# Two issuers for the expert weights: down blocks from GpSimd's queue, up blocks from SyncE's

## What is computed

```
def swiglu(h, w1, w3, w2):
    return (jax.nn.silu(h @ w1) * (h @ w3)) @ w2

def moe_swiglu(h, w_router, w1, w3, w2):
    logits = jnp.einsum('bsd,de->bse', h, w_router)
    top_val, top_idx = lax.top_k(logits, TOP_K)                 # 2 of 8
    top_w = jax.nn.softmax(top_val, axis=-1)
    gates = jnp.sum(one_hot(top_idx, 8) * top_w[..., None], axis=-2)
    out = zeros
    for e in range(8):
        out = out + gates[..., e:e + 1] * swiglu(h, w1[e], w3[e], w2[e])
```

## Time and profile before

| | us |
|---|---|
| median of 3 runs (lowest, highest) | 1298.56 (1297.44, 1298.94) |
| the profiled execution, its own time | 1295.39 |
| its span, first to last instruction | 1293.6 |
| mean granted PE clock over the span | 0.996 |
| expert stage, first block used to last block used | 453.9 to 1282.0 |

### The profile page before, as it was taken

One profiled execution on the slowest core, in us unless ns is written; L12 is line 12 of the kernel. 1 busy time (PEld: TensorE's weight loads), 2 busy tenths in 40 slices (PEclk: granted clock), 3 DMA queues, 4 the chain that ended last, 5 costly groups with the idle time before them and its releaser, 6 DMA issues.

```text
span 1293.6 us, 29466 instructions
## 1 busy us (share of the span) xinstructions
PE 1251.1 (97%) x13303; PEld 732.9 (57%) x13303; DVE 382.4 (30%) x484; ACT 246.3 (19%) x328; POOL 23.0 (2%) x38
## 2 busy tenths in 40 slices
PE   9999999999999999999999999999799999999775
PEld 6998888888999833453433643453243453355222
DVE  4777644444667520111120111002012002011102
ACT  5654543333573300000000000000000000000001
POOL 3000000000100000000000000000000000000000
PEclk9999999999999999999999999999999999999998
DMA  9842745523746899999999999999999999999994
GB/s 312 297 158 98 265 176 174 182 97 116 277 168 235 348 413 404 407 365 414 411 411 412 414 409 413 413 411 411 415 411 412 411 408 406 412 414 397 409 411 202
DMA packets 115972, 430.74 MB, mean 333 GB/s; under 512 B 10615, under 2 KB 17047, under 8 KB 101378
## 3 DMA queue, kind: packets, MB, share of 16 engines
q1 hardware_dynamic: 114226, 423.48, 83.5%
q0 software_dynamic: 1616, 5.33, 1.2%
HBM read 427.72 MB, written 2.11 MB: 332 GB/s over the span
## 4 chain that ended last, share of the span: by engine, by line
PE 87%; DMA 11%; DVE 1%; ACT 1%; issue 0%; SPq 0%; POOL 0%; POOLq 0%; DVEq 0%
PE psum L1907 34%; PE psum L1927 17%; PE psum L1428 9%; PE psum L1430 9%; PE psum L1429 9%; DMA ring<-in_moe_w 9%; PE psum L1644 1%; DMA ring<-in_moe_w_end 1%; PE psum L1881 1%; PE psum L1964 1%; PE psum L1856 1%; PE psum L1447 1%; PE psum L1780 0%; PE psum L1603 0%; PE psum L1604 0%; DMA x<-in_x 0%
## 5 line engine op out<-in xcount | busy, mean ns | idle before, releaser
L1907 PE MATMUL psum<-ring,xe 128*32 128x512 f32 (+1 forms) x5376 | 518.8, 541 | 18.5 <-DMA ring<-in_moe_w 13.5
L1907 PEld LDWEIGHTS psum<-ring,xe 128*32 128x32 f32 x5376 | 168.9, 110 | 348.1 <-issue 271.0
L1927 PE MATMUL psum<-ring,gT 128*32 128x256 f32 x4640 | 259.0, 379 | 9.0 <-DMA ring<-in_moe_w 9.0
L1927 PEld LDWEIGHTS psum<-ring,gT 128*32 128x32 f32 x4640 | 148.1, 110 | 123.3 <-issue 17.2
L1287 DVE TENSOR_TENSOR gate<-gate,psum 128x768 f32<-128x768 f32 (+3 forms) x32 | 24.5, 767 | 511.0 <-ACT gate L831 511.0
L926 DVE TENSOR_TENSOR wlo<-raw,whi 128x2048 fp32r<-128x2048 f32 (+1 forms) x66 | 145.3, 2228 | 58.7 <-ACT whi L657 58.7
L831 ACT ACTIVATE gate<-psum 128x768 f32<-128x768 f32 (+3 forms) x32 | 21.2, 661 | 611.0 <-PE psum L1907 611.0
L657 ACT CAST whi<-raw 128x2048 fp32r<-128x2048 f32 (+1 forms) x66 | 120.2, 1861 | 56.8 <-PE psum L1430 32.5
L1428 PE MATMUL psum<-whi,f_hi 128*128 128x512 f32 (+1 forms) x320 | 123.8, 387 | 1.0 <-DVE wlo L926 0.9
L1430 PE MATMUL psum<-whi,f_lo 128*128 128x512 f32 (+1 forms) x320 | 121.4, 379 | 0.0
L1429 PE MATMUL psum<-wlo,f_hi 128*128 128x512 f32 (+1 forms) x320 | 121.3, 379 | 0.0
(11 more groups left out here) (249 smaller groups left out, 774.1 us busy)
## 6 DMA issues: line engine op xcount, KB each, us to landing
ring<-in_moe_w SPq DMA_DIRECT2D x384, 512.0 KB, 14.9
ring<-in_moe_w SPq DMA_DIRECT2D x112, 1024.0 KB, 18.3
raw<-in_ffn_w SPq DMA_DIRECT2D x33, 1024.0 KB, 5.7
ring<-in_moe_w_end SPq DMA_DIRECT2D x64, 512.0 KB, 16.8
raw<-in_w_mix_in SPq DMA_DIRECT2D x21, 1024.0 KB, 7.4
raw<-in_w_mix_out SPq DMA_DIRECT2D x8, 1024.0 KB, 5.5
raw<-in_w_mix_in SPq DMA_DIRECT2D x4, 544.0 KB, 6.1
x<-in_x SPq DMA_DIRECT2D x2, 512.0 KB, 4.2
```

Of the source, the lines that this page charges most:

```text
L1907: ins = mm(banks(j, n)[o:o + 32, g, 0:2 * q].rearrange("p (i b c) -> p i b c", i=2, c=128), rows_[:, k * CAP + 32 * g:k * CAP + 32 * (g + 1)],
L1927: ins = mm(bank[bk][32 * q:32 * (q + 1), at_:at_ + 256], gT[j % 2][:, a:a + 32], w[:, o:o + 256], start=j == 0 and n == 0 and at_ == 0, st ...
```

## The change

`load_down` moves from SP's program to POOL's. POOL gets a loop over the eight experts (`sweep_downs`) that issues the 14 down blocks of each in PE's order, with the same wait for `moe_used` per block, now an instruction of its own. For each expert but the first POOL loads the expert's number itself. SP keeps the up blocks in their old order. Down blocks signal ten semaphores `down_full` in turn, and no longer the `moe_full` of their slot, and PE waits on these. `free_slot` is the same function, now with the engine as an argument.

```
+DOWNS = 10
-        moe_full = [sem(f"moe_full{i}") for i in range(RING)]
+        moe_full = {i: sem(f"moe_full{i}") for i in range(RING) if i not in (16, 17, 18)}
+        down_full = [sem(f"down_full{i}") for i in range(DOWNS)]
...
         def landings(f):
-            return sum(16 if is_down(g) else 32 for g in range(f % RING, f + 1, RING))
+            return 32 * sum(not is_down(g) for g in range(f % RING, f + 1, RING))
+        def downs(f):
+            return sum(is_down(g) for g in range(f))
...
             # SP
-            def expert(sweep, e, who, turn=0, last=False):
+            def expert(sweep, e, who, last=False):
                 f = PER_SWEEP * sweep + 8 + PER_EXPERT * e
-                load_up(f, who, turn, 1)
-                load_down(f + 8, who, turn, 0)
-                load_up(f + 12, who, turn, 2)
-                load_down(f + 20, who, turn, 1)
-                load_up(f + 24, who, turn, 3)
-                load_down(f + 28, who, turn, 2)
+                load_up(f, who, 0, 1)
+                load_up(f + 12, who, 0, 2)
+                load_up(f + 24, who, 0, 3)
                 if last:
-                    load_down(f + 32, who, turn, 3)
                     return
...
-                load_up(f + 32, then, turn, 0, range(0, 4))
-                load_down(f + 36, who, turn, 3)
-                load_up(f + 34, then, turn, 0, range(4, 8))
+                load_up(f + 32, then, 0, 0, range(0, 4))
+                load_up(f + 34, then, 0, 0, range(4, 8))
...
             # POOL
+            def load_down(f, who, j):
+                w = moe_w2[0].rearrange("e (n p k) d -> n p e k d", p=P, k=4)
+                for b in range(QUARTER[j] // 64):
+                    to, until = free_slot(pool, f + b)
+                    h2 = 2 * (b % 2)
+                    src = w[2 * j + b // 2, :, ds(who, 1), h2:h2 + 2, :].rearrange("p e k d -> p (e k d)")
+                    pool.wait_ge(moe_used, until)
+                    pool.dma_start(to[:, :], src).then_inc(down_full[downs(f + b) % DOWNS], 16)
+            def sweep_downs(sweep):
+                for e in range(EXPERTS):
+                    f = PER_SWEEP * sweep + 8 + PER_EXPERT * e
+                    if e == 1 and sweep == 0:
+                        pool.wait_ge(count_sb, 1)
+                    who = pool.value_load(order[0:1, e:e + 1], min_val=0, max_val=EXPERTS - 1) if e else 0
+                    load_down(f + 8, who, 0)
+                    load_down(f + 20, who, 1)
+                    load_down(f + 28, who, 2)
+                    load_down(f + (36 if e < EXPERTS - 1 else 32), who, 3)
...
             root(3)
             pool.wait_ge(h_ready, 8)
+            sweep_downs(0)
             pool.wait_ge(moe_used, blocks_done(0, PER_EXPERT * (EXPERTS - 2) + 27))
             gains(g_final)
             root(4)
...
             # PE
             def arrived(f, turn):
-                pe.wait_ge(moe_full[ring_slot(f)], landings(f))
+                if is_down(f):
+                    pe.wait_ge(down_full[downs(f) % DOWNS], 16 * (downs(f) // DOWNS + 1))
+                else:
+                    pe.wait_ge(moe_full[ring_slot(f)], landings(f))
```

More of the change, by code:

```diff
@@ L355, in trunk, with free_slot @@
         block = ctx.enter_context(nc.Block())
+        def free_slot(engine, f):
+            slot = ring_slot(f)
+            if 1 <= f < EARLY:
+                engine.wait_ge(lo_ready, MOE0 - RAW_FIXED + f)
+            elif EARLY <= f < EARLY + 6:
+                engine.wait_ge(block_used, MOE0 - SLOTS + 1 + (f - EARLY) // 2)
+            elif EARLY + 6 <= f < EARLY + 6 + ARENA:
+                engine.wait_ge(go_ps, 4)
+            elif EARLY + 6 + ARENA <= f < RING:
+                engine.wait_ge(block_used, MOE0 - SLOTS + 1 + (f - EARLY - ARENA) // 2)
+            return ring[slot], f + 1
         def blocks_done(sweep, p, turn=0):
@@ L474, in dense_chunk @@
                     fill(n + 4 + k, ktiles(rows), 2, D, turn, 6)
[L476 to L487, removed]
             def load_up(f, who, turn, j, some=None):
@@ L492, in load_up @@
                 for b in some or range(KD // nk):
-                    to, until = free_slot(f + b, turn)
+                    to, until = free_slot(sp, f + b)
                     for i, (w, end) in enumerate(((moe_w1, moe_w1_end), (moe_w3, moe_w3_end))):
@@ L501, in load_up @@
                                      ).wait_op(moe_used, until, "sem-ge").then_inc(moe_full[ring_slot(f + b)], 16)
[L503 to L511, removed]
-            def expert(sweep, e, who, turn=0, last=False):
-                f = PER_SWEEP * sweep + 8 + PER_EXPERT * e
-                load_up(f, who, turn, 1)
-                load_down(f + 8, who, turn, 0)
-                load_up(f + 12, who, turn, 2)
-                load_down(f + 20, who, turn, 1)
-                load_up(f + 24, who, turn, 3)
-                load_down(f + 28, who, turn, 2)
+            def expert(sweep, e, who, last=False):
+                f = PER_SWEEP * sweep + 8 + PER_EXPERT * e
+                load_up(f, who, 0, 1)
+                load_up(f + 12, who, 0, 2)
+                load_up(f + 24, who, 0, 3)
                 if last:
-                    load_down(f + 32, who, turn, 3)
                     return
-                if sweep == 0 and isinstance(turn, int):
+                if sweep == 0:
                     sp.wait_ge(count_sb, 1)
-                then = sp.value_load(order[0:1, ds(turn + (e + 1), 1)], min_val=0, max_val=EXPERTS - 1)
-                load_up(f + 32, then, turn, 0, range(0, 4))
-                load_down(f + 36, who, turn, 3)
-                load_up(f + 34, then, turn, 0, range(4, 8))
+                then = sp.value_load(order[0:1, ds(e + 1, 1)], min_val=0, max_val=EXPERTS - 1)
+                load_up(f + 32, then, 0, 0, range(0, 4))
+                load_up(f + 34, then, 0, 0, range(4, 8))
             def chosen_expert(at_):
@@ L641, in _ @@
             with pool.If(count > CAP):
+                for sweep in range(1, SWEEPS):
+                    sweep_downs(sweep)
                 pool.wait_ge(moe_used, blocks_done(SWEEPS - 1, PER_EXPERT * (EXPERTS - 2) + 27))
```

## The result

The changed kernel takes 1314.03 us (median of 4 runs, 1311.11 to 1315.73) against 1298.0 us for the kernel before on the same chip (4 runs, 1297.29 to 1298.94). The ratio is 1.0121, with a 95% interval of 1.01 to 1.0141. The profiled execution took 1314.83 us, with a span of 1313.2 us.

What follows compares the result with a forecast made beforehand. The prediction took the expert stage to be bound by its bytes. Its terms, 0 + 0 + 14.9 + 0 = 14.9 us on 1295.39, gave 1310.3 profiled, 1313.5 for the median, with a range of 1302 to 1365.

Steps and rivals of the forecast that it cites:

- The bound: Expert stage: saturated transfers set the pace, 352.3 MB at 411 GB/s, 857 us.
- The tail: End of the last expert: ups land last, block work follows, PE ends at 1297.0 instead of 1282.05; cost 14.9 us.
- How many downs get ahead, and by when: Last expert: of 20 blocks until 1280.07, 15 are ups and some 5 downs, through by about 1255 with an equal share.
- The comparison of 7.9 with 20.5 us: Issue to landing, `g_final` on POOL's queue against the ring's 1 MB transfers: POOL's transfers do not stand behind SP's.
- The price of two queues: Expert stage: cost of mixing SP's and POOL's queues, between 0 and 75 us, taken as 0; the dear-mixture rival had 0.24.
- The last byte at 1280.07 as before: End of the stage: the same bytes end at the same 1280.07, but the last to land are ups.
- The middle costs nothing: Middle of the stage: engines stay saturated, and PE regains at ready downs what it loses at ups; no cost.
- SP's freed time is worth nothing: Expert stage: taking 112 issues off SP gains nothing; the rival "Faster" had up to 5.8 us, 1292.8, chance 0.06.
- the dip at 549.8: Stretch from 549.8 to 582.1 at 365 GB/s: attributed to a full ring, which stops POOL like SP, so it stays.
- POOL's late start costs nothing: Start of the stage: POOL's first downs come 10.5 us later than SP's, covered by transfers already queued; cost nothing.
- The rival of no difference: Whole stage: only SP's sequencer time is saved, end order unchanged, 1298.6; with partial effects (1296 to 1308) chance 0.18.

Runs made afterwards that it cites:

- e2_last_pool: Against the kernel before, only the last expert's 14 downs go by POOL, the other 98 stay on SP: 1311.84 us, ratio 1.0113.
- e9_last_six: Against the kernel before, only the last expert's last six downs (p 28 to 33) go by POOL: 1307.51 us, ratio 1.0072.
- e10_before_warm: The kernel before with four more idle matmuls (keep_warm) in the routing: 1293.47 us, ratio 0.9980.
- e11_after_warm: The changed kernel with the same four added idle matmuls (keep_warm) in the routing: 1309.98 us, ratio to the kernel before 1.0102.
- e1_last_sp: The changed kernel with the last expert's 14 downs back on SP, the other 98 on POOL: 1297.74 us, ratio to the kernel before 1.0007.
- e3_lead9: The changed kernel with every down held to a lead of 9 blocks on PE instead of 21: 1311.75 us, ratio to the kernel before 1.0125.
- e8_lead15_last: The changed kernel with only the last expert's downs held to a lead of 15 blocks: 1310.08 us, ratio to the kernel before 1.0091.

## Why the prediction was right, point by point

The forecast was 1313.5 us with a range of 1302 to 1365; measured were 1314.03. The main reason held as well, the ups that land last; but two steps in the sum of the tail were wrong and made up for each other.

- **The bound.** Right. The bytes set the pace, and the transfer rate is the same in both kernels.
- **The tail.** Right in mechanism and in size: 14.9 us predicted; the work behind the last landing went from 1.98 to 16.5 us, +14.5, in the order of blocks that was written down (downs p 20 to 23, ups p 24 to 27, the matmul of L1889, six downs). The landing that counts, p 19's, was put at 1269.9 and came at 1274.70, 4.8 us late like the last byte. e2_last_pool (+14.1) and e9_last_six (+10.1 for 10.9 worked out) show it by parts.
- **How many downs get ahead, and by when.** Wrong, and not visible in the sum. Of p 13 to 27 the prediction counts 15 ups; they are 11, the other four being downs. So all ten downs from p 20 on had to land among the ups, not some 5. With ten downs and the equal share that it assumes, ups and downs would have alternated to the end, p 24 to 27 would have landed 5.1 us apart, and by the prediction's own way of counting the cost would be 10.9 us, not 14.9 (an estimate). What restored the 14.9 is the second slip: the share was not equal. The downs had two thirds of the bytes, all ten had landed by 1267.21 (the prediction says about 1255), and only ups were left, 2.55 us apart, p 19 among them. That two errors cancelled here is luck. The comparison of 7.9 with 20.5 us sets 512 KB beside 1 MB; like with like it is 7.9 with 11.0, and for the downs 10.9 with 18.3.
- **The price of two queues,** between 0 and 75 us, taken as 0. Right: 412 GB/s in both, and +0.0 us with 98 downs on POOL. But the earlier trace rows could not show it: with 0.93 of 1.01 MB on POOL's queue it is POOL alone and not a mixture. Taking 0 was a choice that came out well. What slowed was not tried; POOL as the issuer of transfers with rows of 8 KB is ruled out as its cause, its source of a single row of HBM is not shown to be it.
- **The last byte at 1280.07 as before.** Off by 4.7 us in the profiled execution. The step that failed is "The same bytes end at the same 1280.07": I took one profiled execution's start for the kernel's. The clock's stretch at the start is long in some profiled executions and short in others, and moves the end. Against the medians it is less, 16.0 - 14.5 = 1.5 us. With the starts alike (e10_before_warm, e11_after_warm) the step holds, 1279.48 and 1279.02; there the term that is missing is the lower clock behind PE's waits for ups, 2.9 us in the profiled execution.
- **The middle costs nothing.** Right for the time, e1_last_sp, but the reason given was too kind. PE does not regain all of it; it carries a lag, and e1_last_sp ends with PE and the bytes level. With a lag of a few us more it would have cost.
- **SP's freed time is worth nothing, and the dip at 549.8 is the full ring's.** Right. The dip stayed (355 GB/s), and so did the full ring: from 540 to 582 us SP waits 30.5 us for PE to free a slot, 28.0 before. In e3_lead9 the dip is absent.
- **POOL's late start costs nothing.** It began its first downs at 446.80, and 413 GB/s were moved around it. Right.
- **The rival of no difference** (sequencer time only). It describes e1_last_sp exactly: 98 transfers moved, +0.0 us. The Trainium skill ("DMA: Bandwidth & Descriptors", section "Issuing engines are not separate DMA queues") says that issuing from several engines saves only the sequencer's time. This case agrees as long as the end of the stage keeps its order (1.0007); with the order changed the measurement is another, 1.0121, and it decides.

What I expected of e3_lead9 was wrong because the start of the stage was left out, as with the late last byte: a limit that looks at the end of the stage was applied to the whole of it, and the start, which needs the opposite, was not looked at.

## What to carry to other kernels

One queue that is filled in the order of need is also a schedule: in the kernel before, bytes landed in that order. If some of a stream goes to a second queue, it can overtake the rest by as many buffers as are free. Where the transfers are the bound, the cost is the work that stands behind the last landing for which the computing engine has to wait; read it off by listing that work. Keep the last ring's worth of transfers on one queue, which cost nothing here (e1_last_sp). To limit the lead there is second best (+3.8 us), and it must be there only: at the start the ring must be allowed to fill.

## What the runs showed of the hardware that I had not expected

Two queues with work shared the engines packet for packet, not byte for byte: 1310 and 1281 packets, 9.45 and 4.66 MB from 1230 to 1264 us. The queue with the longer rows got the larger part of the rate. Rows of the same length on both queues were not tried.

SP, with all blocks on its queue, was 9 blocks ahead of PE at the end, 12 transfers, though 21 buffers stood open; the rest of its lead it could not use. What holds an issue back there was not tried. In the last 8 us or so of transfers the DMA share halves (0.49 to 0.53, 197 to 217 GB/s) in both kernels. It would fit if half of the 16 engines had finished earlier, but the trace does not tell the engines apart. Two stretches, one of each kernel:

```profile
1276.00:1278.00 2.00, 1.38 (x29) 0.61 (x22) 0.00 (x0) 0.00 (x0) 0.00 (x0) 1.00 0.49 205
```

```profile
1278.00:1280.00 2.00, 2.00 (x44) 1.23 (x40) 1.22 (x2) 0.00 (x0) 0.00 (x0) 1.00 0.52 197
```

The first is before, the second after. The cause was not tried and stays open; at half the rate for that long it is worth some 4 us to both (an estimate). And a stretch of low clock of 10 to 14 us in the routing, ahead of all expert work, goes with a last byte 2 to 5 us later, 800 us on: 1282.21, 1283.13, 1284.77 and 1285.04 (e2_last_pool, e9_last_six, the change, e8_lead15_last) against 1280.07. From 582 us on the engines run at 409 to 415 GB/s in both kernels, so there is no room in which to make good the lost bytes.
